# Turned tiles fetched by ScalarE three slots behind the block transpose, and parameter pieces seven blocks later

## What is computed

```python
for l in range(2):                                   # hybrid_layer
    u = rms_norm(x, norm_g[l]); p = u @ w_in[l]      # 2048 x 16400
    y_a = norm(mlstm(conv(q, k), v, i, f) * sigmoid(o)) * g * silu(z_a)
    y_b = rg_lru(conv(xb)) * silu(z_b)
    x = x + concat(y_a, y_b) @ w_out[l]
x = rms_norm(x, final_g); mem_n = rms_norm_2(mem)
for i, kind in enumerate("ABCA"):
    z = rms_norm_2(x, norm_g_2[i]) @ w_in_kind
    mix = {"A": gmlp_spatial_gating, "B": forgetting_attention,
           "C": differential_attention}[kind](...)
    kv = mem_n @ w_mem_kv_2[i]                       # the four of these run first
    x = x + concat(mix, memory_attention(mq, mk, mv)) * silu(gate) @ w_out_2[i]
```

## Time and profile before

| | us |
|---|---|
| median of three runs (3237.38 to 3238.11) | 3237.96 |
| profiled execution | 3238.11 |
| its span | 3236.3 |
| PE busy | 3221.1 |
| DVE busy | 2157.9 |
| ACT busy | 1707.4 |
| POOL busy | 324.6 |

### The profile page before, as it was taken

How to read it: one execution, slowest core, us unless ns; L and a number is a source line. 1 busy time by engine, 2 the same in 40 slices (tenths; PEclk the granted TensorE clock), 3 DMA queues, 4 the chain that set the end, 5 groups by cost and what they waited for, 6 DMA issues and landing times.

```text
span 3236.3 us, 39270 instructions
## 1 busy us (share of the span) xinstructions
PE 3221.1 (100%) x14828; PEld 2679.6 (83%) x14828; DVE 2157.9 (67%) x2951; ACT 1707.4 (53%) x2338; POOL 324.6 (10%) x506
## 2 busy tenths in 40 slices
PE   8999999999999999999999999999999999999999
PEld 7888888888888888888888888888888888888887
DVE  5559665657768666657678666666666687767564
ACT  5546444547755544546756454454545555545453
POOL 1100000000010000000010000011100233210000
PEclk9999999999999999999999999999999999999999
DMA  7877666676676666667677666767657666676665
GB/s 257 274 234 230 209 198 197 202 225 189 198 248 214 209 213 200 215 188 223 199 237 238 182 220 212 226 209 224 206 183 253 211 205 197 195 264 213 187 204 175
DMA packets 338124, 692.82 MB, mean 214 GB/s; under 512 B 26332, under 2 KB 28548, under 8 KB 337552
## 3 DMA queue, kind: packets, MB, share of 16 engines
q1 hardware_dynamic: 311888, 617.75, 59.9%
q0 software_dynamic: 23648, 66.26, 6.7%
q10 hardware_dynamic: 2400, 6.30, 0.5%
HBM read 646.90 MB, written 43.32 MB: 213 GB/s over the span
## 4 chain that ended last, share of the span: by engine, by line
PE 97%; DVE 1%; DMA 1%; issue 0%; ACT 0%; POOL 0%; SPq 0%; ACTq 0%; DVEq 0%; POOLq 0%
PE acc L1758 30%; PE acc L1760 30%; PE acc L1759 30%; PE nm L1952 1%; DMA weights_raw<-in_a_w_in_dram 1%; DVE weights_lo L1299 1%; PE tr L1760 0%; PE tr L1758 0%; PE tr L1940 0%; PE tr L1759 0%; PE sc L1926 0%; PE sc L1917 0%; PE tr L1834 0%; ACT weights_hi L979 0%; PE tr L1952 0%
## 5 line engine op out<-in xcount | busy, mean ns | idle before, releaser
L1299 DVE TENSOR_TENSOR weights_lo<-weights_raw,weights_hi 128x1024 fp32r<-128x1024 f32 x1103 | 1344.3, 1227 | 832.3 <-ACT weights_hi L979 826.5
L979 ACT ACTIVATE weights_hi<-weights_raw 128x1024 fp32r<-128x1024 f32 x1103 | 1160.9, 1058 | 1154.2 <-PE acc L1760 1022.3
L1758 PE MATMUL acc<-weights_hi,u_hi 128*128 128x512 f32 x3136 | 1235.2, 394 | 0.5 <-DVE weights_lo L1299 0.5
L1760 PE MATMUL acc<-weights_hi,u_lo 128*128 128x512 f32 x3136 | 1222.2, 390 | 0.0
L1759 PE MATMUL acc<-weights_lo,u_hi 128*128 128x512 f32 x3136 | 1221.1, 389 | 0.0
L1758 PEld LDWEIGHTS acc<-weights_hi,u_hi 128*128 128x128 f32 x3136 | 588.8, 188 | 125.2 <-issue 4.0
L1760 PEld LDWEIGHTS acc<-weights_hi,u_lo 128*128 128x128 f32 x3136 | 588.6, 188 | 123.7
L1759 PEld LDWEIGHTS acc<-weights_lo,u_hi 128*128 128x128 f32 x3136 | 588.9, 188 | 120.1
L1758 PE MATMUL acc<-weights_hi,y_hi 128*128 128x512 f32 x1278 | 500.5, 392 | 7.4 <-DVE work L1438 6.4
L1760 PE MATMUL acc<-weights_hi,y_lo 128*128 128x512 f32 x1278 | 498.6, 390 | 0.0
L1759 PE MATMUL acc<-weights_lo,y_hi 128*128 128x512 f32 x1278 | 498.3, 390 | 0.0
(11 more groups left out here) (265 smaller groups left out, 2004.0 us busy)
## 6 DMA issues: line engine op xcount, KB each, us to landing
weights_raw<-in_w_in_dram SPq DMA_DIRECT2D x384, 512.0 KB, 4.2
weights_raw<-in_w_out_dram SPq DMA_DIRECT2D x256, 512.0 KB, 4.5
weights_raw<-in_a_w_in_dram SPq DMA_DIRECT2D x176, 512.0 KB, 4.5
weights_raw<-in_b_w_in_dram SPq DMA_DIRECT2D x112, 512.0 KB, 3.8
weights_raw<-in_c_w_in_dram SPq DMA_DIRECT2D x112, 512.0 KB, 4.0
weights_raw<-in_w_mem_kv_dram SPq DMA_DIRECT2D x63, 512.0 KB, 5.2
turn_scratch_uq<-work POOLq DMA_DIRECT2D x80, 128.0 KB, 3.1
work<-turn_scratch_uq SPq DMA_DIRECT2D x20, 512.0 KB, 6.1
```

The source lines that it names most:

```text
L979: SC_E.activation(WH[:, b % RING], RAW[:, b % RING], ACT.Copy).then_inc(sem("hi_done"), 1)
L1299: V.tensor_tensor(WL[:, b % RING], RAW[:, b % RING], WH[:, b % RING].bitcast(F32), ALU.subtract).then_inc(sem("lo_done"), 1)
L1758: T.matmul(dst, hi_l, hi_r, start=start, stop=False, **kw)
L1760: return T.matmul(dst, lo_l, hi_r, start=False, stop=stop, **kw)
```

## The change

The fetch of a turned tile moves from SP's queue to ACT's, with the same waits and the same DMA. `FETCH` is 3 where it was 11, so ACT comes to it in the third slot behind the flip, after that slot's split. The five parameter pieces move to later slots: `params` and `params_log` by seven, `params_in` by eight, `tbias` and `tb_store` by twelve.

```diff
-FETCH, JOIN, LOW = 11, 8, 1
+FETCH, JOIN, LOW = 3, 8, 1
...
-    pl.piece(FIRST + 11, "params")
-    pl.piece(FIRST + 12, "params_log")
-    pl.piece(FIRST + 13, "params_in")
-    pl.piece(FIRST + 14, "tbias")
-    pl.piece(FIRST + 15, "tb_store")
+    pl.piece(FIRST + 18, "params")
+    pl.piece(FIRST + 19, "params_log")
+    pl.piece(FIRST + 21, "params_in")
+    pl.piece(FIRST + 26, "tbias")
+    pl.piece(FIRST + 27, "tb_store")
...
@block.sync
-                for p in pl.at[n]:
-                    if p.kind == "fetch":
-                        ... (the same waits)
-                        sp.wait_ge(sem("spilled_" + LANE[p.buf]), 64 * (p.nth + 1))
-                        sp.dma_start(turned(p.buf), SPILL[LANE[p.buf]].rearrange("b r a e -> (b r) (a e)")
-                                     ).then_inc(sem("fetched_" + LANE[p.buf]), 16)
...
@block.scalar
+                    elif k == "fetch":
+                        if p.buf in ("q", "x"):
+                            wait(act, "cj_out", p.at.last.get("cjoin"))
+                        elif p.buf == "n":
+                            wait(act, "qt_out", p.at.last.get("qt"))
+                        else:
+                            wait(act, "jn_lo", p.at.last.get(("low", p.buf)))
+                        act.wait_ge(sem("spilled_" + LANE[p.buf]), 64 * (p.nth + 1))
+                        act.dma_start(turned(p.buf), SPILL[LANE[p.buf]].rearrange("b r a e -> (b r) (a e)")
+                                      ).then_inc(sem("fetched_" + LANE[p.buf]), 16)
```

## The result

The changed kernel takes 3250.68 us (median of five, 3249.51 to 3255.28) where the kernel before, in the same comparison, takes 3237.43: a ratio of 1.0042 with a 95% interval of 1.0032 to 1.0053. It is slower by 13.3 us. The prediction was 3240.1, no change beyond 0.2%, with a range up to 3246; the time lies above it. The span of the profiled execution grew from 3236.3 to 3248.9, 12.6 us.

A forecast was written before the change was run, and what follows sets the result against it. PE bounds the kernel, busy 3221.1 of 3236.3 us. Part one gains 6.2 us and part two loses 8.2, net +2.0 on the profiled execution's 3238.11: 3240.1 us, no change beyond 0.2%, range 3232.5 to 3246.

The forecast's parts named there:

- The parameters: Part one, first stall before block 16: moving the parameter pieces later gains 4.57 + 2.5 − 0.9 = 6.2 us.
- an idle time of 2.9 us lies inside the 4.3 us through which the clock stayed up: First stall: the remaining idle time leaves PE's clock at 1.00, so 2.5 us of half-speed loss count as gained.
- The second rival: First stall: the clock falls in the remaining 2.9 us idle, 2.5 us are not gained, total 3242.6; chance 0.12.
- The table's matmuls: Two matmuls, free during the first stall, stand twelve blocks later in a full stream and cost 0.8 to 0.9 us.
- Lane um: Eight flips in the two mLSTM layers: ACT's wait for spills stalls PE by 3.2 us in all, 2 to 5.
- Differential attention: Spill waits delay ACT's splits and squares: stalls of 2.4 us at group 1 to 2, 1.2 at 0 to 1.
- the spill lands at 2752.60: Differential attention, group 1 to 2: landing time from which the chain to PE's 2.4 us stall is counted.
- 9.0 us: Differential attention: time from spill landing through issue, split, squares, power and L1438, used at both group changes.
- part two: 70 fetches moved from SP to ACT, eight slots earlier: 3.2 + 2.4 + 1.2 + 1.4 = 8.2 us lost, ends 4 to 13.
- Last gMLP layer: DMA-limited stretch: the fetch goes ahead of weight loads, about 1.4 us of stall, 0 if queues serve otherwise.
- the waits never reach PE: Rival: buffers hide ACT's waits, most of the 8.2 us vanishes, total 3231.9 up to 3235; chance 0.18.
- SP, no longer held: Rival: SP's weight loads delay spills at nine places, some 9 us per us of delay, beyond 3244.6; chance 0.15.

The follow-up runs named there:

- e11: The changed kernel with only lane n's fetch (first tile of each attention group) back on SP at slot + 11: 3248.72 us, ratio 1.0034.
- e7: The kernel with only the parameters moved, plus one unneeded VectorE pass over 128x1024 right behind the instruction releasing POOL's first head-norm power: 3231.97 us, single run.
- e8: The changed kernel with SP waiting for the spill at its old fetch place (slot + 11), issuing nothing: 3250.40 us, ratio 1.0038.
- e6: The kernel with only the parameters moved, VectorE making the low half of ten blocks again in 5 to 8 extra passes, to stall PE; no time given.

## Why the prediction was wrong, point by point

- **What bounds the kernel**: right. PE is the bound, and each us found is idle time or half speed of PE.
- **The parameters**: right in kind and nearly in size (4.6 us by the medians, 5.5 in the profile, 6.2 forecast). Two errors of the working nearly cancel: the power was taken at 2.57 us and took 1.67 (1.0 more gained with what follows), and of the 2.5 us for the clock 1.6 were not gained, since it fell all the same. The step that failed here is "an idle time of 2.9 us lies inside the 4.3 us through which the clock stayed up". I looked at the clock during the idle time; here it falls after PE has begun again. The second rival held in part in this execution, behind an even shorter stall, and the sign that the prediction names for it, a half-speed stretch near 60 us, is there. What I had not considered: the clock also fell behind two of the stalls that the change makes.
- **The table's matmuls**: 1.0 us where 0.8 to 0.9 were forecast.
- **Lane um**: right in mechanism, places and nearly in size, 4.8 us for 3.2. The landings were taken as they were; the fifth flip's came 0.7 us later (9.4 us after the first store for 8.7), which is within what the traces show for this flip with its fetch on SP (8.2 to 9.8 us).
- **Differential attention**: right in mechanism and chain, wrong by a factor of three, and this makes the sum wrong. The forecast was 1.2 + 2.4. The spills came 1.2 and 1.4 us later (early fetch of the other tile, e11), each power took 0.9 more (order against DVE's split, e7 for the mechanism), and the two stretches at half speed cost 1.6 us each: 3.6 + 2.6 + 1.8 + 3.2 = 11.2, of which 0.4 come back ahead of block 945, against 10.9. So three steps failed. The landing ("the spill lands at 2752.60") and the power's 2.93 within the "9.0 us" were carried over from the trace of before as constants, though the change alters what runs beside them. And the clock behind the stalls that part two itself forecasts was put at nothing, without a reason.
- **Last gMLP layer**: right, 1.2 for 1.4. **Other lanes**: 1.1 us up to block 597, where I had none.
- **The rivals**: "the waits never reach PE" fell. "SP, no longer held" named the right effect, late spills, with the wrong cause: e8 shows no change with SP held. Its nine places were too many: beside the two of the attention, only two um flips, the second and the fifth, have the spill later, by 0.6 and 0.7 us.
- **The range**: its upper end, 3246, rested on the bound of 13 us for part two; the measured 18 lies outside because none of the bounds allowed the terms to move together, and they do: ACT's wait also makes the order that lengthens the power (3.83 us in e11 too, where the spills are on time), and the longer stall can bring down the clock.

## What to carry to other kernels

A DMA moved to a compute engine's queue is cheap to issue and dear to wait for: look at when its semaphore is due, compare with when that engine gets there, and put it behind the work that others wait for; here one slot for ab alone takes all but 2.5 of the 13 us away, and two slots for all lanes turn the loss of 13 us into a gain of 5. When a wait delays a chain, don't carry the chain's durations over: ask of each term what runs beside it at its new time. A us taken from PE's idle time may be worth more or less than one, as the clock goes; count it as a chance, not as a sure gain.

## What the runs showed of the hardware

- The granted clock can fall to 0.50 some 0.5 to 1.5 us after a short stall is over, with PE at work; all eight falls behind stalls of 1.9 to 3.0 us are such, while of the stalls of 3.3 us and more some had it before they ended. It came back after 3.4 us here, where after the stall of 6.35 us before it took at least 5.1 us of work. Whether it falls after a stall of 2 us isn't the same from one execution to the next.
- A POOL power of 128x8 or 128x16 values takes 0.9 us more when a two-input DVE pass over 128x1024 has started 0.17 us ahead of it, and nothing more when that pass starts behind it (1.67 and 2.57, 2.93 and 3.83 us) or when the pass ahead is a block transpose with one input (1.64).
- A spill of four 128 KB stores of the lane ab landed after 7.9 to 9.0 us when a 512 KB load from the scratch n went out within 0.6 us of its first store, and after 6.8 to 7.5 us, but for one of 7.9, when that load went out 1.9 to 2.4 us behind it (e6 left out, where one at 2.4 us took 8.5). At the um flips a load from the scratch uq that goes out within 0.9 us of the first store shows less: 6.0 to 8.4 us, where those with it 1 to 4 us later took 5.5 to 7.3.
